# A two-layer transformer program on one core: two more pairs of heads turned by VectorE, values merged in twos, three more low parts by adding DMAs

## The reference, cut to what matters

```python
s = einsum('bqgrd,bkgd->bgrqk', q_i, k_i) * SCALE - slopes[:, :, None, None] * dist
p = masked_softmax(s, mask)
return einsum('bgrqk,bkgd->bqgrd', p.astype(v_i.dtype), v_i)   # p must be turned: keys on the partitions
...
proj = xn @ w_in      # the projections that run beside it, and lend the engines their time
```

## Time and profile before

| what | value |
|---|---|
| median of 3 runs | 902.04 us (901.62 to 902.25) |
| profiled execution, its own time | 901.26 us |
| its span in the trace | 899.2 us |
| PE busy | 892.7 us (99%) |
| DVE busy | 706.0 us (79%) |
| ACT busy | 555.3 us (62%) |
| POOL busy | 43.2 us (5%) |
| granted clock of PE, mean over the span | 0.999 of full |

### The profile page before, as it was taken

One profiled execution on the slowest core, in us unless ns is written; L12 is line 12 of the kernel. 1 busy time (PEld: TensorE's weight loads), 2 busy tenths in 40 slices (PEclk: granted clock), 3 DMA queues, 4 the chain that ended last, 5 costly groups with the idle time before them and its releaser, 6 DMA issues.

```text
span 899.2 us, 13582 instructions
## 1 busy us (share of the span) xinstructions
PE 892.7 (99%) x4926; PEld 767.0 (85%) x4926; DVE 706.0 (79%) x1381; ACT 555.3 (62%) x954; POOL 43.2 (5%) x54
## 2 busy tenths in 40 slices
PE   9999999999999999999999999999999999999997
PEld 7988877888888888888889998888889988888886
DVE  6888899789866666677998999999976786666665
ACT  7767878755644444456655657776745755754454
POOL 0410000000000000000010100100000000000000
PEclk9999999999999999999999999999999999999999
DMA  9977677676465555556798888487565377555551
GB/s 343 320 214 199 177 203 219 198 293 202 154 229 187 192 191 196 190 191 209 219 236 268 231 206 270 106 230 240 169 211 164 114 212 237 187 187 187 188 188 47
DMA packets 97218, 184.53 MB, mean 205 GB/s; under 512 B 8128, under 2 KB 18176, under 8 KB 96896
## 3 DMA queue, kind: packets, MB, share of 16 engines
q1 hardware_dynamic: 92128, 166.35, 56.1%
q0 software_dynamic: 4656, 16.78, 10.0%
q10 hardware_dynamic: 368, 0.52, 0.2%
HBM read 164.69 MB, written 1.05 MB: 184 GB/s over the span
## 4 chain that ended last, share of the span: by engine, by line
PE 99%; ACT 1%; issue 0%; DVE 0%; DVEq 0%; ACTq 0%
PE pb L523 97%; PE pb L527 1%; PE pb L738 1%; ACT SM L1400 0%; ACT wlo L1174 0%; ACT SM L1174 0%; ACT whi L1174 0%; ACT PTC L1174 0%; DVE XS L2617 0%; DVE XS L2625 0%; DVEq L59 0%; DVE DG L2359 0%; ACT MSQ L1757 0%; DVE ST L2603 0%; ACT CC L1174 0%
## 5 line engine op out<-in xcount | busy, mean ns | idle before, releaser
L1174 ACT ACTIVATE whi<-raw 128x1024 fp32r<-128x1024 f32 (+2 forms) x304 | 309.1, 1039 | 125.5 <-PE pb L523 112.5
L1787 DVE TENSOR_TENSOR wlo<-raw,whi 128x1024 fp32r<-128x1024 f32 (+1 forms) x267 | 315.7, 1211 | 78.7 <-ACT whi L1174 78.2
L523 PE MATMUL pb<-XT,whi 128*128 128x512 f32 (+1 forms) x1232 | 283.8, 358 | 0.0
L523 PE MATMUL pb<-whi,ZO 128*128 128x512 f32 (+1 forms) x776 | 238.9, 388 | 0.0
L523 PEld LDWEIGHTS pb<-XT,whi 128*128 128x128 f32 x1232 | 200.8, 189 | 23.8 <-issue 1.4
L523 PEld LDWEIGHTS pb<-whi,ZO 128*128 128x128 f32 x776 | 145.2, 188 | 29.7 <-issue 0.4
L523 PE MATMUL pb<-XT,wlo 128*128 128x256 f32 (+1 forms) x1032 | 166.4, 282 | 0.0
L523 PEld LDWEIGHTS pb<-XT,wlo 128*128 128x128 f32 (+1 forms) x1032 | 153.2, 190 | 14.0
L523 PE MATMUL pb<-whi,XT 128*128 128x512 f32 (+1 forms) x544 | 161.8, 389 | 0.0
L523 PE MATMUL pb<-wlo,ZO 128*128 128x512 f32 (+1 forms) x388 | 148.3, 387 | 0.0
L523 PEld LDWEIGHTS pb<-whi,XT 128*128 128x128 f32 x544 | 101.0, 188 | 20.7 <-issue 0.7
(11 more groups left out here) (258 smaller groups left out, 657.9 us busy)
## 6 DMA issues: line engine op xcount, KB each, us to landing
raw<-in_w_in SPq DMA_DIRECT2D x105, 512.0 KB, 4.8
raw<-in_w_ff SPq DMA_DIRECT2D x64, 512.0 KB, 5.3
raw<-in_w_up SPq DMA_DIRECT2D x32, 512.0 KB, 4.5
raw<-in_w_down SPq DMA_DIRECT2D x32, 512.0 KB, 4.8
wlo<-raw POOLq DMA_DIRECT2D x31, 512.0 KB, 5.8
raw<-in_w_branch_b SPq DMA_DIRECT2D x8, 512.0 KB, 5.3
raw<-in_w_out SPq DMA_DIRECT2D x8, 512.0 KB, 4.1
raw<-in_wx_kv SPq DMA_DIRECT2D x8, 512.0 KB, 5.4
```

The lines of the kernel that those rows point to most:

```text
L523: return e.matmul(o, l, r, start=start, stop=stop, skip_group_check=True)
L1174: return e.activation(o, i, ACT.Copy, scale=scale)
L1787: e.tensor_tensor(wlo[u % NW][:, 0:c], raw_tile(u)[:, 0:c], whi[u % NW][:, 0:c].bitcast(F32), ALU.subtract).then_inc(lo, 1)
```

## The change

Four things are altered. (1) Pairs 1 and 2 (items 2 to 5) are now turned by DVE in the same way as pairs 3 to 7, in two portions each instead of three: 10 and 6 instructions for pair 1 at steps 18 and 19, 8 and 8 for pair 2 at steps 21 and 22. PE turns items 0 and 1 alone, and a third `PT` buffer is added. (2) The values of the eight pairs are summed in twos, at steps 22, 29, 35 and 42. (3) ACT scales item 0 at step 13 instead of 14. (4) The units 27, 31 and 34 get their low parts by an adding DMA: 27 and 31 are the last units of `b1_x1` and `b1_b0`, 34 is the third of `b1_b1`.

```diff
-        PTP = [work(W0 + a, f"PT{i}", 768) for i, a in enumerate((12016, 14840))]
+        PTP = [work(W0 + a, f"PT{i}", 768) for i, a in enumerate((12016, 14840, 7216))]
...
+        def pt1(j):
+            return PTP[j // 2 % 3][:, 384 * (j % 2):384 * (j % 2) + 384]
...
-        by_dma = [22, 25, 29, 33, 36, 39, 42, 45, 48, 51, 54]
+        by_dma = [22, 25, 27, 29, 31, 33, 34, 36, 39, 42, 45, 48, 51, 54]
...
-        values_of = {a: (i,) for i, a in enumerate(pair_at[3:] + (35,))}
-        values_of[42] = (6, 7)
-        last_value = {a: n[-1] // 2 for a, n in values_of.items() if n[-1] % 2}
-        blocks_of = {pair_at[n] + 5 + i: (n, i) for n in (3, 4, 5, 6, 7) for i in range(3)}
-        by_pe = [j for j in range(16) if j // 2 not in (3, 4, 5, 6, 7)]
+        values_of = {22: (0, 1), 29: (2, 3), 35: (4, 5), 42: (6, 7)}
+        last_value = {a: n[0] // 2 for a, n in values_of.items()}
+        blocks_of = {pair_at[n] + 5 + i: (n, a, b) for n in (3, 4, 5, 6, 7)
+                     for i, (a, b) in enumerate(((0, 6), (6, 11), (11, 16)))}
+        blocks_of[pair_at[1] + 5], blocks_of[pair_at[1] + 6] = (1, 0, 10), (1, 10, 16)
+        blocks_of[pair_at[2] + 5], blocks_of[pair_at[2] + 6] = (2, 0, 8), (2, 8, 16)
+        by_pe = [0, 1]
...
-                    if s - 4 in pair_of:
+                    if s == 13:
+                        scale_p(0, 0)
+                    if s - 4 in pair_of and s > 14:
                         scale_p(2 * pair_of[s - 4], 0)
...
                     if s in blocks_of:
-                        n, part = blocks_of[s]
-                        if part == 0:
+                        n, first_block, end_block = blocks_of[s]
+                        if first_block == 0:
                             e.wait_ge(sc_p, 2 * n + 2)
-                            e.wait_ge(pv_done, 2 * n - 2)
-                        for m in range((0, 6, 11)[part], (6, 11, 16)[part]):
+                            if n > 2:
+                                e.wait_ge(pv_done, 2 * n - 4)
+                        for m in range(first_block, end_block):
```

More of the change, by code:

```diff
@@ L106, in build @@
         SMP = [work(W0 + 10480 + 768 * i, f"SM{i}", 768) for i in range(2)]
-        PTP = [work(W0 + a, f"PT{i}", 768) for i, a in enumerate((12016, 14840))]
+        PTP = [work(W0 + a, f"PT{i}", 768) for i, a in enumerate((12016, 14840, 7216))]
         SM, PT = ([v[i // 2][:, 384 * (i % 2):384 * (i % 2) + 384] for i in range(4)] for v in (SMP, PTP))
-        SM2, PT2 = ([v[i][:, :].rearrange("p (c n) -> p c n", c=6) for i in range(2)] for v in (SMP, PTP))
+        SM2, PT3 = ([v[:, :].rearrange("p (c n) -> p c n", c=6) for v in b] for b in (SMP, PTP))
+        def pt1(j):
+            return PTP[j // 2 % 3][:, 384 * (j % 2):384 * (j % 2) + 384]
         CC = [work(W0 + a, f"CC{i}", 1024)[:, :].rearrange("p (f n) -> p f n", f=4) for i, a in enumerate((12784, 16240))]
@@ L903, in attention1 @@
                         for p in range(2):
-                            mm(PB[7][64 * p:64 * p + 64, 0:256], QKV[:, 0, v0:v0 + 64], PT[(2 * n + p) % 4][:, 0:256],
+                            mm(PB[7][64 * p:64 * p + 64, 0:256], QKV[:, 0, v0:v0 + 64], pt1(2 * n + p)[:, 0:256],
                                b == 0, False)
@@ L907, in attention1 @@
                             mm(PB[7][64 * p:64 * p + 64, 128:256], QKV[:, 1, v0:v0 + 64],
-                               PT[(2 * n + p) % 4][:, 256:384], False, False).then_inc(pv_done, 1)
+                               pt1(2 * n + p)[:, 256:384], False, False).then_inc(pv_done, 1)
                         if b == 1:
@@ L1412, in copy_p @@
                 e.wait_ge(pt_done, len(by_pe) + j + 1 if base else by_pe.index(j) + 1)
-                if base + j >= 4:
+                if base:
                     e.wait_ge(pv_done, base + j - 3)
-                copy(PT[j % 4][:, :], PB[5 if base else 6][:, 0:384]).then_inc(pt_out, 1)
+                elif j >= 6:
+                    e.wait_ge(pv_done, j - 5)
+                copy(PT[j % 4] if base else pt1(j), PB[5 if base else 6][:, 0:384]).then_inc(pt_out, 1)
             def make_o_hi(p, bank, done, c=0):
@@ L2064, in attention1 @@
                     if s in blocks_of:
-                        n, part = blocks_of[s]
-                        if part == 0:
+                        n, first_block, end_block = blocks_of[s]
+                        if first_block == 0:
                             e.wait_ge(sc_p, 2 * n + 2)
-                            e.wait_ge(pv_done, 2 * n - 2)
-                        for m in range((0, 6, 11)[part], (6, 11, 16)[part]):
+                            if n > 2:
+                                e.wait_ge(pv_done, 2 * n - 4)
+                        for m in range(first_block, end_block):
                             a, b = m // 4 * 32, m % 4 * 32
-                            i = e.transpose(PT2[n % 2][b:b + 32, :, a:a + 32], SM2[n % 2][a:a + 32, :, b:b + 32])
-                        if part == 2:
+                            i = e.transpose(PT3[n % 3][b:b + 32, :, a:a + 32], SM2[n % 2][a:a + 32, :, b:b + 32])
+                        if end_block == 16:
                             i.then_inc(p_blocks, 1)
```

## The result

The changed kernel takes 910.19 us at the median of 6 runs (909.71 to 913.61), the kernel before 901.96 us (901.62 to 902.5): a ratio of 1.0098, 95% interval 1.0082 to 1.0113. It is slower by 8.2 us. The profiled execution took 909.71 us, with a span of 907.8.

A forecast was written before the change was run, and what follows sets the result against it. PE's list was taken to bound the kernel, with DVE's late additions setting the time after the change. 901.26 + 6.1 (DVE's delay) + 2.0 (clock) = 909.4 profiled, 910.0 us at the median; range 904.5 to 912.5.

The forecast's parts named there:

- The two meetings: Where DVE's additions free banks for PE, units 32 and 36: PE waits 2.4 and 5.3 us there.
- DVE's queue: DVE's list from 93.9 us: added turns delay additions to 102.9 and 122.6; unit 36 starts 6.1 us later.
- PE's own list: Turns, merges and item 0's wait leave PE: 2.3 us together; PE reaches unit 32's bank at 100.9.
- The clock: PE's granted clock falls after the 5.3 us wait ahead of unit 36, costing 2.0 us.
- the second bank: At unit 36, free 0.8 us after the first, wanted after 0.45: 0.35 us more.
- The merges: Three merges of values on PE save 0.15 us each, 0.45; the two later ones give back 0.3.
- rival (d): Whole kernel: gain and waits cancel, 902.0 us, needing waits of 2.3 instead of 8.3; chance 0.04.
- the lower bound of +5.2: Low end of the +5.2 to +8 us given for DVE's delay; counting unit 31's whole 1.14 takes 0.6 off.
- Rival (a): Same waits at units 32 and 36 but no fall of the clock: 908.1 us; chance 0.28.
- (c): DVE catches up in part, only one of the two waits counts: +2 to +4, 905 us; chance 0.09.
- (e): DVE or an adding DMA makes PE late at a third place behind unit 36: above 912.5 us; chance 0.05.
- Rival (b): DVE's additions aren't late and PE's 2.3 us gain is kept: 899.7 us; chance 0.06.

The follow-up runs named there:

- e7: Changed kernel with the old list of low parts, so DVE makes those of units 27, 31 and 34 again; 911.53 us.
- e3: Changed kernel with pair 1 turned by PE again, pair 2 staying with DVE; 908.55 us.
- e4: Changed kernel with pairs 1 and 2 both turned by PE again; merges, earlier scale and added low parts by DMA stay; 902.01 us.
- e5: Kernel before with only the merged values and item 0's earlier scale; 901.66 us.
- e1: Changed kernel with idle products on PE, 9 ahead of unit 32 and 20 ahead of unit 36; 908.66 us.
- e11: e2 run once more, unaltered; distance +1.60 us in its trace, three of ten executions at 904.45 to 905.09 us.
- e10: e3 with 20 idle products on PE ahead of unit 36; 906.76 us.
- e8: Changed kernel with pair 2 by PE, pair 1's turns split 12 and 4, low parts 31, 34, 35, 37 by DMA (27 not), ACT's copy moved earlier; 901.05 us.
- e2: Changed kernel with pair 2 turned by PE again, pair 1 staying with DVE; 903.73 us.

## Why the prediction was right

Forecast 910.0, measured 910.19. The two meetings decided the change, in the way and with nearly the sizes that the text gives. Step by step:

- **DVE's queue.** First addition of `b1_b0` 102.9 forecast, 103.30 in the trace; from there to that of `b1_b1` 19.7 forecast, 19.71 in the trace; unit 36 +6.1 forecast, +6.62 in the trace. Of the 0.5 between, 0.4 is in the first leg and 0.1 in the hand-over from the addition to unit 36 (0.57, where I had 0.45). The three low parts relieve DVE by 1.0 (e7), where I had 1.64: unit 27 is not 0 but -0.94, since ACT's added copy makes the exponentials late that DVE waits for, unit 31 is 1.13 instead of 0.5, as ACT's copies were done at 90.82 and not at 91.3, and unit 34 is 0.80 instead of 1.14. The 19.7 was right for a reason that I had in part wrong: the idle 0.93 lies ahead of pair 2's turns, which can't fill it (e3, where it grew to 1.49); DVE was simply late there from the first meeting.
- **PE's own list.** PE was to reach unit 32 at 100.9 and did so at 101.43 (103.97 - 2.54). The 0.5 is what the low parts cost at the banks of unit 28 (e4 against e5, 0.48). It fell into the wait.
- **The clock.** One fall was forecast, after the second wait, at 2.0 us; after the wait of 2.4 I had none. Here a step failed: the clock fell after the first wait too (2.54), and unit 32 took long. It cost nothing only because DVE was late at unit 36 anyway: it turned the second wait from 5.3 into 3.8, which is why the waits add up to 6.3 and not 8. The fall in unit 36 measured 1.6 (e1), mis-sized by 0.4; the second bank came as forecast, 0.38 (3.11 in e1 against 2.73 before) where I had 0.35. My price came from the slow products at the program's start. The window of the kernel before, below, gives the granted clock as 1.00 there, so the record doesn't show that the lower clock made them slow:

```profile
5.00:6.00 1.00, 1.00 (x3) 0.78 (x3) 0.91 (x2) 0.32 (x2) 0.00 (x0) 1.00 1.04 350
```

- **The merges** gave their share: with item 0's wait 0.8 was forecast, but alone they give 0.3 by the distance (e5), since a turn then waits 0.51 for ACT's copy. In the changed kernel those turns aren't there.
- **The sum** against the trace's 8.35: 6.62 (unit 36), 0.38 (second bank: 3.11 - 2.73), 1.6 (clock), less 0.3 for the last merges, is 8.3. That the forecast of 910.0 is met to 0.2 is in part luck: the start of unit 36 was 0.5 later than the sum has it, and the fall 0.4 cheaper. Two numbers of the text do not fit its own sum: the waits of rival (d), 8.3, are 2.4 + 5.3 + 0.35 = 8.05, and the lower bound of +5.2 is 6.1 - 0.6 = 5.5. Neither moves the forecast.

Rival (a), no fall, is what e1 comes nearest to: 908.66 measured, 908.1 forecast for (a). Rivals (c), (d) and (e) didn't come: the second wait is 3.78 and not under 3, gain and waits don't cancel, and PE waits for nothing behind unit 36. Rival (b), the gain kept, rested on a turning instruction of 0.11 us. The trace after has 112 of them at 369 ns:

```profile
L2082 DVE STREAM_TRANSPOSE PT<-SM 32x192 f32<-32x192 f32 x112 | 41.4, 369 | 1.6
L1876 DVE STREAM_TRANSPOSE HB<-GB 32x256 f32<-32x256 f32 x16 | 7.0, 436 | 0.2
```

The Trainium skill (VectorE: DVE Perf Modes, The three transpose paths and Rules for kernel authors) calls VectorE the fastest for blocks of 32x32 and has 311 ns for a bf16 tile of 128x128; a pair here is 128 x 768 in float32 and 16 instructions, and measured 6.1 us. By that figure the change pays, by the trace it doesn't. (The same rules send a turn of a whole 128x128 tile to TensorE, and the traces side with that: an item, three such tiles, costs 0.31 to 0.42 us of PE's list and a copy of some 0.5 by ACT, or 3.05 of DVE's.)

By the distances, at full clock: pair 1 alone on DVE +1.6 (e11), pair 2 alone +4.7 (e10), both +6.8 (e1), and the clock's fall 1.6 on top makes the 8.35.

## What to carry to other kernels

Work that goes to an engine with a fifth of its time free is paid for at the next place where another engine waits for it: count the idle time between the last two such meetings, and only the idle that lies behind the added work in its list, or behind a lateness that the engine brings along. The same 16 instructions cost 1.6 us in one place and 4.7 in another. Cut into 12 and 4 around a meeting, with four low parts taken from the engine instead of three and one copy of ACT moved, they cost nothing that could be seen (e8; what each of these three edits gives was not measured). When TensorE comes to wait, price the clock as well, but only where nothing later hides it: a slow unit ahead of a second wait was free.

## What was not expected of the hardware

A TensorE wait of 1.6 to 1.7 us was followed by the lower clock in one traced execution and not in another of the same program (e2, e11). The fall may come in the wait or behind it: in e3 the windows of its wait of 5.15 us (from 116.9) show 0.82 in 119 to 120 and 0.50 from 120; in the changed kernel the clock was still 1.00 in the last window of the wait of 3.78, 0.64 in 124 to 125 and 0.50 from 125 on, with PE at work. Two lengths of DVE's turning instruction are in the trace, 369 ns for 192 numbers a partition and 436 for 256: an estimated 1.05 ns for each number and 168 ns for the instruction itself. If that line holds, nearly half of a turn of six blocks does not depend on its size; it rests on two points, taken from instructions at different places.
